# RMS norms without Sqrt: pow on GpSimd, and the FFN's output epilogue spread over four steps

## The chip, the cores and the metric

The kernel runs on all 8 cores of one Trainium2 chip, each with its own part of the batch and no exchange between them. The metric is the device time in microseconds of the slowest core for one execution.

## The reference

One layer of an encoder over 24 sequences (8 and 16 in two batches) of 2048 tokens and width 1024. For each sequence:

```python
h = rms_norm(x, g_mix_pre) * (1 + sc1) + sh1
x = x + gt1 * rms_norm(token_mixer(h), g_mix_post)      # two attention branches, sigmoid gates, w_out
h = rms_norm(x, g_ffn_pre) * (1 + sc2) + sh2
x = x + gt2 * rms_norm(conv_ffn(h), g_ffn_post)         # w_up, conv of width 3, gelu(gate)*val, w_down

def rms_norm(x, g):
    return x * lax.rsqrt(mean(x * x, axis=-1, keepdims=True) + EPS) * g
```

The token mixer is `w_out @ (sigmoid(ga) * ya + sigmoid(gb) * yb)`, where ya and yb are a mixture of three dilated window attentions and a neighbourhood attention on a 32 x 64 grid, 8 heads of 64 each. The FFN has 2816 channels (`D_FF`), so w_up has 5632 columns. Outputs are in float32.

## The kernel before

Each core takes three sequences one after the other (loop over `s`). For each sequence the stages are, with a barrier of all engines between them: the first norm with transposes into `hT` (`ln_to_hT`, four blocks `tcn` of 512 tokens); the two attention branches; the output of the mixer (L746 to L810, four blocks `tcn`); the second norm (`ln_to_hT` again); the FFN (from L826, four blocks `tcn`).

All instructions are recorded by `P.add(engine, ...)` in program order. Each engine executes its own in that order; `reads` and `writes` of the small `Res` objects become semaphore waits of the recorded instruction. A waiting instruction holds up everything recorded behind it on its engine. GpSimd ("pool") has no arithmetic here: its queue holds the weight loads (`wload`, L345), 1 MB of bf16 for eight 128-row pieces of 512 columns. A load waits until the last matmul that reads its slot's former weights is done. Slots come from rings: in the mixer's output `ringC` has three slots and six loads per block (two gate weights at c=0, one at c=2, one at c=4, the two halves of w_out at c=6 and behind c=7); in the FFN `ringF` has four slots, and loads come in pairs (value and gate) at j = 0, 4, 8, 12, 16, 20, then six for w_down.

Mixer output, per block: for c = 0 to 7 TensorE computes ya and yb (L764) and the two gate projections (L781), ScalarE the two Sigmoids (L788, L789), VectorE the products and their sum. Then for each of four 128-token tiles (tt) 16 matmuls with w_out (L807), and `residual_epilogue` (L934) reads the two PSUM halves.

FFN, per block: for j = 0 to 21 TensorE computes the value and the gate half of channel group j (L849, 16 matmuls, two of six PSUM banks); ScalarE scales and biases the middle tap (L866) and mends the block's edges (L871, L875); VectorE adds the two outer taps in place (L881, L885), which frees the banks; one step later come ScalarE's Gelu (L890) and VectorE's product (L892). Then the down-projection (L906) and its copies to SBUF, `RB` (L911). The epilogue of a block is kept in `pend_epi` and recorded in the next block, at j == 3, all four tiles in one go: two Squares with sums (L943), an add (L945), Sqrt (L947), reciprocal (L949), then per half a scaling (L951) and the residual add (L954), and the store of the tile by SP's queue (L920). The first block of a sequence has none pending; the last block's epilogue is recorded at the sequence's end.

`ln_to_hT` has the same pattern per block: four Squares (L434), one Sqrt of 128x4 (L436), reciprocal (L438), four scalings (L440), then 32 transposes (L445). The function tables of ScalarE are switched by the build where the next function isn't in the loaded set: Exp and Ln share one, Sigmoid, Gelu and Sqrt are in others; Square and Identity cause no switch.

Of the kernel before, what the change touches and what calls it, by code (L numbers as in the profile page):

```python
# [6 lines left out]
F32 = mybir.dt.float32  # L7
BF16 = mybir.dt.bfloat16
AF = mybir.ActivationFunctionType
ALU = mybir.AluOpType  # L10
# [4 lines left out]
D = 1024  # L15
NSEQ = 3
NEG = -240000.0
EPS = 1e-6
# [195 lines left out]
def build(debug=False):  # L214
# [16 lines left out]
    P = Prog(nc)  # L231
    A = nc.alloc_sbuf_tensor
# [197 lines left out]
    def ln_to_hT(src_tiles, src_res, tcn, sc_ap, sh_ap, inplace_dst, r_xn):  # L430
        r_ss, r_rs, r_rs2 = r_lnst[tcn % 2]
        so = 4 * (tcn % 2)
        for tt in range(4):
            P.add("act", lambda e, tt=tt: e.activation(out=junk[:], in_=src_tiles[tt], func=AF.Square,  # L434
                                                      accum_out=stat[:, so + tt:so + tt + 1]), reads=[src_res], writes=[r_ss])
        P.add("act", lambda e: e.activation(out=stat[:, 8 + so:12 + so], in_=stat[:, so:so + 4], func=AF.Sqrt, scale=1.0 / D, bias=epsb[:, 0:1]),  # L436
              reads=[r_ss], writes=[r_rs])
        P.add("dve", lambda e: e.reciprocal(out=stat[:, 16 + so:20 + so], in_=stat[:, 8 + so:12 + so]), reads=[r_rs], writes=[r_rs2])  # L438
# [17 lines left out]
    epsb = A("epsb", [128, 1], F32)  # L456
    P.add("dve", lambda e: e.memset(epsb[:], EPS), writes=[r_const])
    r_vec = Res()
    hT_all = [r_hT[j][t] for j in range(8) for t in range(4)]

    def x1tile(i):
        return RA[:, i * D:(i + 1) * D]

    for s in range(nseq):
# [284 lines left out]
        for tcn in range(4):  # L749
# [50 lines left out]
            for tt in range(4):  # L800
                i = tcn * 4 + tt
                pss = []
                for hf in range(2):
                    ps, rps = nb()
                    pss.append((ps, rps))
                    for k in range(8):
                        P.add("pe", lambda e, ps=ps, k=k, tt=tt, hf=hf, wo=wo: e.matmul(  # L807
                            ps[:], lhsT=gT[:, k * 512 + tt * 128:k * 512 + tt * 128 + 128], rhs=wsl(wo[hf][0], k, 512, 0, 512),
                            start=(k == 0), stop=(k == 7)), reads=[r_mg, wo[hf][1]], writes=[rps])
                residual_epilogue(P, pss, x1tile(i), r_x, gt1bc, r_bc, stat, junk, epsb, r_const, Res())  # L810
# [16 lines left out]
        for tcn in range(4):  # L827
            pend = None
            for j in range(22):
# [9 lines left out]
                if j == 3 and pend_epi[0] is not None:  # L839
                    pend_epi[0]()  # L840
                    pend_epi[0] = None
# [71 lines left out]
            def epi(tcn=tcn, s=s, mo_res=mo_res):  # L913
                for tt in range(4):
                    i = tcn * 4 + tt
                    r_y = Res()
                    residual_epilogue(P, [(RB[:, tt * D: tt * D + 512], mo_res[tt]), (RB[:, tt * D + 512: tt * D + 1024], mo_res[tt])],
                                      x1tile(i), Res(), gt2bc, r_bc, stat, junk, epsb, r_const, r_y, sb=True)
                    dsty = bass.AP(y_d, (s * S + i * 128) * D, [[D, 128], [1, D]])
                    P.add("sp", lambda e, dsty=dsty, i=i: e.dma_start(out=dsty, in_=x1tile(i)), reads=[r_y], dma=True)  # L920
            pend_epi[0] = epi
        pend_epi[0]()
# [8 lines left out]
_rst = [None]  # L931


def residual_epilogue(P, halves, xt, r_x, gbc, r_bc, stat, junk, epsb, r_const, r_out, sb=False):  # L934
    if _rst[0] is None:
        _rst[0] = [Res() for _ in range(4)]
# [5 lines left out]
    for hf, (src, rps) in enumerate(srcs):  # L942
        P.add("act", lambda e, src=src, hf=hf: e.activation(out=junk[:, 0:512], in_=src, func=AF.Square,  # L943
                                                            accum_out=stat[:, 32 + c + hf:33 + c + hf]), reads=[rps], writes=[r_st])
    P.add("dve", lambda e: e.tensor_tensor(out=stat[:, 34 + c:35 + c], in0=stat[:, 32 + c:33 + c], in1=stat[:, 33 + c:34 + c], op=ALU.add),  # L945
          reads=[r_st], writes=[r_st])
    P.add("act", lambda e: e.activation(out=stat[:, 35 + c:36 + c], in_=stat[:, 34 + c:35 + c], func=AF.Sqrt, scale=1.0 / D, bias=epsb[:, 0:1]),  # L947
          reads=[r_st, r_const], writes=[r_st])
    P.add("dve", lambda e: e.reciprocal(out=stat[:, 48 + ci:49 + ci], in_=stat[:, 35 + c:36 + c]), reads=[r_st], writes=[r_st])  # L949
# [63 lines left out]
```

How the kernel before makes its waits and increments, by code:

```python
            def run(e, eng):  # L123
                waited = {}
                for x in self.q[e]:
                    for d in x.deps:
                        if d.dma:
                            key = (d.qkey, d.slot)
                            val = d.slotcnt
                            if waited.get(key, 0) >= val:
                                continue
                            waited[key] = val
                            eng.wait_ge(dsem[d.qkey][d.slot], 16 * val)
                        else:
                            key = d.eng
                            val = d.cnt
                            if waited.get(key, 0) >= val:
                                continue
                            waited[key] = val
                            eng.wait_ge(csem[d.eng], val)
                    if x.fn is None:
                        continue
                    bi = x.fn(eng)
                    if x.dma:
                        bi.then_inc(dsem[x.qkey][x.slot], 16)
                    elif x.sig:
                        bi.then_inc(csem[e], 1)
```

## Time and profile before

| what | us |
|---|---|
| median of 2 runs | 5241.87 |
| the two runs | 5103.49 and 5380.25 |
| profiled execution, its own time | 5114.34 |
| its span (slowest core, core 2) | 5112.8 |
| spans of the 8 cores | 5088.2 to 5112.8 |
| busy: TensorE, VectorE, ScalarE, GpSimd | 3720.7, 2231.6, 2419.8, 357.9 |

A time is that of the whole execution; the span runs from the first to the last instruction of a core. All rows are of core 2. PE is TensorE, DVE VectorE, ACT ScalarE, POOL GpSimd, SP the queue of SyncE. In a timeline each row is one or more like instructions in a row; what stands in brackets is how long the engine was idle before them and whose end released it. PEclk is the granted TensorE clock as a share of 2.4 GHz. Some matmul records are missing (63 for 64, say).

### The profile page before, as it was taken

How to read it: one execution, taken by the hardware profiler on the slowest of the kernel's cores; microseconds unless marked ns; L12 is line 12 of the kernel's file. 1: busy time of each engine (PE TensorE's matmuls, PEld its weight loads, DVE VectorE, ACT ScalarE, POOL GpSimd, SP SyncE). 2: the span in 40 equal slices, each digit the busy share in tenths (PEclk: the TensorE clock that was granted, in tenths of full speed). 3: DMA queues.
4: the chain of work that ended last, by engine and by line, in shares of the span. 5: the costliest groups of instructions: out<-in, count | busy, mean ns of one | idle time of the engine just before them, and what ended most of it. 6: DMA issues, size and time to landing. Idle time of an engine off the chain costs nothing.

```text
span 5112.8 us, 67412 instructions; the slowest of 8 cores (5088.2 to 5112.8 us)
## 1 busy us (share of the span) xinstructions
PE 3720.7 (73%) x20982; PEld 1953.1 (38%) x21288; DVE 2231.6 (44%) x3231; ACT 2419.8 (47%) x4878; POOL 357.9 (7%) x417
## 2 busy tenths in 40 slices
PE   1277777795998827777688589973777758958887
PEld 1144444333443324444333344432454433333343
DVE  1444400344566654440034456664543003455665
ACT  0244566224566524556522456652455652245664
POOL 1000000000111000000000011100000000001110
PEclk9689998897999959999889799986999989979998
DMA  8934250521444330000143144433000023224443
GB/s 113 177 50 60 34 75 9 171 99 57 142 149 135 124 122 15 9 13 11 40 142 102 51 152 149 144 112 118 13 7 13 13 64 128 91 66 136 153 149 107
DMA packets 150410, 450.05 MB, mean 88 GB/s; under 512 B 8496, under 2 KB 52528, under 8 KB 149680
## 3 DMA queue, kind: packets, MB, share of 16 engines
q0 software_dynamic: 126160, 356.18, 26.8%
q1 hardware_dynamic: 23904, 89.54, 5.0%
q8 instruction: 182, 2.98, 0.2%
q14 instruction: 164, 1.34, 0.1%
HBM read 468.40 MB, written 57.15 MB: 103 GB/s over the span
## 4 chain that ended last, share of the span: by engine, by line
PE 58%; ACT 14%; issue 9%; DVE 9%; DMA 8%; ACTq 0%; DVEq 0%; POOL 0%; SPq 0%; POOLq 0%
PE pb L849 11%; PE pb L906 9%; PE pb L557 6%; PE pb L781 5%; PE pb L617 5%; PE pb L638 5%; DMA wr<-w_in_bf 5%; PE pb L620 3%; PE pb L807 3%; PE pb L523 3%; PE pb L764 3%; PE pb L445 2%; ACT junk L434 2%; ACT RA L625 2%; DMA RA<-x 2%
## 5 line engine op out<-in xcount | busy, mean ns | idle before, releaser
L625 ACT ACTIVATE RA<-pb 128x448 bf16<-128x448 f32 (+5 forms) x1248 | 543.2, 467 | 269.6 <-PE pb L620 151.3
L617 PE MATMUL pb<-RA 128*128 128x256 bf16 (+4 forms) x2148 | 599.1, 315 | 39.6 <-DVE RA L593 28.9
L881 DVE SCALAR_TENSOR_TENSOR attA<-pb,spt,attA 128x511 f32<-128x511 f32 x528 | 382.5, 747 | 454.9 <-PE pb L849 231.6
L849 PE MATMUL pb<-hT,wr 128*128 128x512 bf16 x2052 | 489.9, 391 | 114.1 <-DVE attA L885 85.4
L638 PE MATMUL pb<-RA 128*128 128x256 bf16 (+5 forms) x2160 | 415.3, 267 | 215.2 <-ACT RA L625 187.3
L849 PE MATMUL pb<-hT,attB 128*128 128x512 bf16 x2067 | 472.6, 382 | 45.4 <-DVE attA L885 42.9
L866 ACT ACTIVATE attA<-pb,spt 128x512 f32<-128x512 f32 x528 | 391.7, 770 | 71.6 <-PE pb L849 70.9
L885 DVE SCALAR_TENSOR_TENSOR attA<-pb,spt,attA 128x511 f32<-128x511 f32 x528 | 368.9, 740 | 0.0
L557 PE MATMUL pb<-hT,wr 128*128 128x512 bf16 x1488 | 359.1, 390 | 8.5 <-ACT RA L547 5.6
L715 DVE TENSOR_TENSOR attB<-pb,RA 64x512 bf16<-64x512 f32 x96 | 66.1, 688 | 655.8 <-ACT RA L713 655.8
L849 PEld LDWEIGHTS pb<-hT,wr 128*128 128x128 bf16 x2112 | 205.3, 100 | 360.2 <-issue 140.8
L638 PEld LDWEIGHTS pb<-RA 128*128 128x128 bf16 x2160 | 193.3, 105 | 366.5 <-issue 308.5
L620 PE MATMUL pb<-Tb,identb 128*128 128x192 bf16 (+2 forms) x1296 | 317.2, 268 | 0.0
L781 PE MATMUL pb<-hT,wr 128*128 128x512 bf16 x1128 | 275.0, 390 | 57.1 <-DMA wr<-w_in_bf 52.8
L849 PEld LDWEIGHTS pb<-hT,attB 128*128 128x128 bf16 x2112 | 203.0, 98 | 283.1 <-issue 51.8
L617 PEld LDWEIGHTS pb<-RA 128*128 128x128 bf16 x2160 | 247.2, 116 | 109.6 <-issue 50.8
L523 PE MATMUL pb<-hT,wr 128*128 128x512 bf16 x744 | 172.2, 389 | 117.0 <-DMA wr<-w_in_bf 106.3
L906 PE MATMUL pb<-wr,RC 128*128 128x512 bf16 x1035 | 235.4, 386 | 15.4 <-DVE attA L885 14.3
L345 POOL DMA_DIRECT2D wr<-w_in_bf x108 | 95.7, 887 | 2105.9 <-PE pb L523 1156.2
L906 PE MATMUL pb<-attB,RC 128*128 128x512 bf16 x1035 | 231.9, 382 | 5.2 <-DVE attA L885 4.1
L911 ACT ACTIVATE RC<-pb 128x512 f32<-128x512 f32 x96 | 57.3, 597 | 374.1 <-PE pb L906 374.1
L668 DVE TENSOR_TENSOR RA<-pb,RA 128x512 f32<-128x512 f32 x96 | 105.8, 1102 | 279.0 <-ACT RA L664 239.0
(130 smaller groups left out, 5447.4 us busy)
## 6 DMA issues: line engine op xcount, KB each, us to landing
wr<-w_up_bf POOLq DMA_DIRECT2D x60, 1024.0 KB, 6.2
attB<-w_up_bf POOLq DMA_DIRECT2D x60, 1024.0 KB, 6.7
RA<-x SPq DMA_DIRECT2D x24, 2048.0 KB, 20.1
wr<-w_in_bf POOLq DMA_DIRECT2D x36, 1024.0 KB, 5.9
wr<-w_down_bf POOLq DMA_DIRECT2D x24, 1024.0 KB, 7.7
attB<-w_down_bf POOLq DMA_DIRECT2D x24, 1024.0 KB, 7.7
y<-RA SPq DMA_DIRECT2D x48, 512.0 KB, 2.6
wr<-w_in_bf POOLq DMA_DIRECT2D x72, 256.0 KB, 3.9
```

The costliest lines, as they stand in the source:

```text
L523: P.add("pe", lambda e, ps=ps, k=k, tcn=tcn, wt=wt: e.matmul(ps[:], lhsT=wsl(wt, k, 128, 0, 128), rhs=hT[:, k * S + tcn * 512:k * S + tcn ...
L557: P.add("pe", lambda e, ps=ps, k=k, tcn=tcn, wt=wt: e.matmul(ps[:], lhsT=wsl(wt, k, 128, 0, 128), rhs=hT[:, k * S + tcn * 512:k * S + tcn ...
L617: P.add("pe", lambda e, ps=ps, col=col, nq=nq, lk=lk, rq=rq: e.matmul(ps[:, col:col + nq], lhsT=lk, rhs=rq, start=True, stop=False, skip_g ...
L620: P.add("pe", lambda e, ps=ps, col=col, nq=nq, mrhs=mrhs: e.matmul(ps[:, col:col + nq], lhsT=identb[:], rhs=mrhs, start=False, stop=True, ...
L625: P.add("act", lambda e, ex=ex, ps=ps, col=col: e.activation(out=ex, in_=ps[:, 0:col], func=AF.Exp, scale=0.125), reads=[rps], writes=[r_e ...
L638: P.add("pe", lambda e, bk=bk, ac0=ac0, nq=nq, lv=lv, exs=exs, first=first: e.matmul(accb[bk][:, ac0:ac0 + nq], lhsT=lv, rhs=exs, start=fi ...
L781: P.add("pe", lambda e, ps_=ps_, w_=w_, k=k, tcn=tcn, c=c: e.matmul(ps_[:], lhsT=wsl(w_, k, 512, (c % 4) * 128, 128), rhs=hT[:, k * S + tc ...
L849: P.add("pe", lambda e, ps=ps, k=k, wt=wt, tcn=tcn, ncol=ncol, jj=jj: e.matmul(ps[:], lhsT=wsl(wt, k, ncol, jj * 128, 128), rhs=hT[:, k * ...
L866: P.add("act", lambda e, t=bufs[isg], ps=mains[isg][0], w1=cw[isg][1], cb=cw[isg][3]: e.activation(out=t, in_=ps[:], func=AF.Identity, sca ...
L881: P.add("dve", lambda e, t=bufs[isg], ps=mains[isg][0], w0=cw[isg][0]: e.scalar_tensor_tensor(out=t[:, 1:512], in0=ps[:, 0:511], scalar=w0 ...
L885: P.add("dve", lambda e, t=bufs[isg], ps=mains[isg][0], w2=cw[isg][2]: e.scalar_tensor_tensor(out=t[:, 0:511], in0=ps[:, 1:512], scalar=w2 ...
L906: P.add("pe", lambda e, ps=ps, k=k, kk=kk, tt=tt, wt=wt: e.matmul(ps[:], lhsT=gT[:, k * 512 + tt * 128:k * 512 + tt * 128 + 128], rhs=wsl( ...
```

## The change

The Sqrt on ScalarE and the reciprocal on VectorE become a `tensor_scalar` on VectorE (times 1/D, plus EPS) and a `tensor_tensor` with `pow` on GpSimd, whose exponent is a small tile `mhalf` of -0.5; in `ln_to_hT` (24 calls) as in `residual_epilogue` (96 calls). The Squares of the epilogues now also write a common resource `r_junk`. The epilogue of an FFN block, recorded in the next one, is no longer all at j == 3 but one tile each at j = 2, 5, 8 and 11. The mixer's epilogues and the one at a sequence's end stay where they are.

```diff
--- before.py
+++ after.py
@@ -433,9 +433,10 @@
         for tt in range(4):
             P.add("act", lambda e, tt=tt: e.activation(out=junk[:], in_=src_tiles[tt], func=AF.Square,
                                                       accum_out=stat[:, so + tt:so + tt + 1]), reads=[src_res], writes=[r_ss])
-        P.add("act", lambda e: e.activation(out=stat[:, 8 + so:12 + so], in_=stat[:, so:so + 4], func=AF.Sqrt, scale=1.0 / D, bias=epsb[:, 0:1]),
-              reads=[r_ss], writes=[r_rs])
-        P.add("dve", lambda e: e.reciprocal(out=stat[:, 16 + so:20 + so], in_=stat[:, 8 + so:12 + so]), reads=[r_rs], writes=[r_rs2])
+        P.add("dve", lambda e: e.tensor_scalar(out=stat[:, 8 + so:12 + so], in0=stat[:, so:so + 4], scalar1=1.0 / D, scalar2=EPS,
+                                               op0=ALU.mult, op1=ALU.add), reads=[r_ss], writes=[r_rs])
+        P.add("pool", lambda e: e.tensor_tensor(out=stat[:, 16 + so:20 + so], in0=stat[:, 8 + so:12 + so], in1=mhalf[:, 0:4], op=ALU.pow),
+              reads=[r_rs, r_const], writes=[r_rs2])
         for tt in range(4):
             P.add("dve", lambda e, tt=tt: e.tensor_scalar(out=inplace_dst[tt], in0=src_tiles[tt], scalar1=stat[:, 16 + so + tt:17 + so + tt],
                                                           scalar2=None, op0=ALU.mult), reads=[src_res, r_rs2], writes=[r_xn])
@@ -454,7 +455,9 @@
                                                                         op0=ALU.mult, op1=ALU.add), reads=[rps, r_vec], writes=[r_hT[j][tcn]])
 
     epsb = A("epsb", [128, 1], F32)
+    mhalf = A("mhalf", [128, 4], F32)
     P.add("dve", lambda e: e.memset(epsb[:], EPS), writes=[r_const])
+    P.add("dve", lambda e: e.memset(mhalf[:], -0.5), writes=[r_const])
     r_vec = Res()
     hT_all = [r_hT[j][t] for j in range(8) for t in range(4)]
 
@@ -807,7 +810,7 @@
                         P.add("pe", lambda e, ps=ps, k=k, tt=tt, hf=hf, wo=wo: e.matmul(
                             ps[:], lhsT=gT[:, k * 512 + tt * 128:k * 512 + tt * 128 + 128], rhs=wsl(wo[hf][0], k, 512, 0, 512),
                             start=(k == 0), stop=(k == 7)), reads=[r_mg, wo[hf][1]], writes=[rps])
-                residual_epilogue(P, pss, x1tile(i), r_x, gt1bc, r_bc, stat, junk, epsb, r_const, Res())
+                residual_epilogue(P, pss, x1tile(i), r_x, gt1bc, r_bc, stat, junk, mhalf, r_const, Res())
         P.barrier()
 
         dump('x1', RA[:])
@@ -836,9 +839,10 @@
                 ffs[0] += 1
                 bufs = (attAf[:, st_ * 1024: st_ * 1024 + 512], attAf[:, st_ * 1024 + 512: st_ * 1024 + 1024])
                 ph, rph = pb[6 + j % 2], rb[6 + j % 2]
-                if j == 3 and pend_epi[0] is not None:
-                    pend_epi[0]()
-                    pend_epi[0] = None
+                if j in (2, 5, 8, 11) and pend_epi[0] is not None:
+                    pend_epi[0]((j - 2) // 3)
+                    if j == 11:
+                        pend_epi[0] = None
                 mains = []
                 for isg in range(2):
                     wt, wr_ = (tv_, tg_)[isg]
@@ -910,16 +914,16 @@
                     ps, rps = pss[tt]
                     P.add("act", lambda e, ps=ps, tt=tt, hf=hf: e.activation(out=RB[:, tt * D + hf * 512: tt * D + hf * 512 + 512], in_=ps[:], func=AF.Identity),
                           reads=[rps], writes=[mo_res[tt]])
-            def epi(tcn=tcn, s=s, mo_res=mo_res):
-                for tt in range(4):
+            def epi(tt_sel, tcn=tcn, s=s, mo_res=mo_res):
+                for tt in ([tt_sel] if tt_sel is not None else range(4)):
                     i = tcn * 4 + tt
                     r_y = Res()
                     residual_epilogue(P, [(RB[:, tt * D: tt * D + 512], mo_res[tt]), (RB[:, tt * D + 512: tt * D + 1024], mo_res[tt])],
-                                      x1tile(i), Res(), gt2bc, r_bc, stat, junk, epsb, r_const, r_y, sb=True)
+                                      x1tile(i), Res(), gt2bc, r_bc, stat, junk, mhalf, r_const, r_y, sb=True)
                     dsty = bass.AP(y_d, (s * S + i * 128) * D, [[D, 128], [1, D]])
                     P.add("sp", lambda e, dsty=dsty, i=i: e.dma_start(out=dsty, in_=x1tile(i)), reads=[r_y], dma=True)
             pend_epi[0] = epi
-        pend_epi[0]()
+        pend_epi[0](None)
         pend_epi[0] = None
         P.barrier()
     P.barrier()
@@ -931,9 +935,10 @@
 _rst = [None]
 
 
-def residual_epilogue(P, halves, xt, r_x, gbc, r_bc, stat, junk, epsb, r_const, r_out, sb=False):
+def residual_epilogue(P, halves, xt, r_x, gbc, r_bc, stat, junk, mhalf, r_const, r_out, sb=False):
     if _rst[0] is None:
-        _rst[0] = [Res() for _ in range(4)]
+        _rst[0] = [Res() for _ in range(5)]
+    r_junk = _rst[0][4]
     ci = _ctr[0] % 4
     c = ci * 4
     _ctr[0] += 1
@@ -941,12 +946,13 @@
     srcs = [(ps if sb else ps[:], rps) for (ps, rps) in halves]
     for hf, (src, rps) in enumerate(srcs):
         P.add("act", lambda e, src=src, hf=hf: e.activation(out=junk[:, 0:512], in_=src, func=AF.Square,
-                                                            accum_out=stat[:, 32 + c + hf:33 + c + hf]), reads=[rps], writes=[r_st])
+                                                            accum_out=stat[:, 32 + c + hf:33 + c + hf]), reads=[rps], writes=[r_st, r_junk])
     P.add("dve", lambda e: e.tensor_tensor(out=stat[:, 34 + c:35 + c], in0=stat[:, 32 + c:33 + c], in1=stat[:, 33 + c:34 + c], op=ALU.add),
           reads=[r_st], writes=[r_st])
-    P.add("act", lambda e: e.activation(out=stat[:, 35 + c:36 + c], in_=stat[:, 34 + c:35 + c], func=AF.Sqrt, scale=1.0 / D, bias=epsb[:, 0:1]),
+    P.add("dve", lambda e: e.tensor_scalar(out=stat[:, 35 + c:36 + c], in0=stat[:, 34 + c:35 + c], scalar1=1.0 / D, scalar2=EPS,
+                                           op0=ALU.mult, op1=ALU.add), reads=[r_st], writes=[r_st])
+    P.add("pool", lambda e: e.tensor_tensor(out=stat[:, 48 + ci:49 + ci], in0=stat[:, 35 + c:36 + c], in1=mhalf[:, 0:1], op=ALU.pow),
           reads=[r_st, r_const], writes=[r_st])
-    P.add("dve", lambda e: e.reciprocal(out=stat[:, 48 + ci:49 + ci], in_=stat[:, 35 + c:36 + c]), reads=[r_st], writes=[r_st])
     for hf, (src, rps) in enumerate(srcs):
         P.add("dve", lambda e, src=src, hf=hf: e.scalar_tensor_tensor(out=src, in0=src, scalar=stat[:, 48 + ci:49 + ci],
                                                                    in1=gbc[:, hf * 512:(hf + 1) * 512], op0=ALU.mult, op1=ALU.mult),
```

## Rows read from the trace of the kernel before

**Rows 1.** Page, chain that ended last: share of span by engine.
```profile
PE 58%; ACT 14%; issue 9%; DVE 9%; DMA 8%; ACTq 0%; DVEq 0%; POOL 0%; SPq 0%; POOLq 0%
```

**Rows 2.** ScalarE by line: name, shape, count | busy us, mean ns | idle.
```profile
L947 ACT ACT_TABLE_LOAD x24 | 30.8, 1283 | 15.3 <-DVE stat L945 15.3
...
L788 ACT ACT_TABLE_LOAD x12 | 15.4, 1283 | 95.3 <-PE pb L781 95.2
L890 ACT ACT_TABLE_LOAD x12 | 15.4, 1283 | 0.2
L436 ACT ACTIVATE stat<-stat,epsb 128x4 f32<-128x4 f32 x24 | 7.1, 297 | 2.8
```

**Rows 3.** Waits: who waited <- for whom: us total, times, longest.
```profile
PE pb L849 <- DVE attA L885: 128.2, 9, 14.6
```

**Rows 4.** Timeline, second FFN block: start, duration us, engine, line [idle <-releaser].
```profile
3032.14 13.98 PE L849 MATMUL pb<-hT,attB 128*128 128x512 bf16 x63
...
3037.49 1.51 DVE L881 SCALAR_TENSOR_TENSOR attA<-pb,spt,attA 128x511 f32<-128x511 f32 x2 [37.85 <-PE pb L849]
...
3040.95 1.51 DVE L881 SCALAR_TENSOR_TENSOR attA<-pb,spt,attA 128x511 f32<-128x511 f32 x2 [0.63 <-ACT attA L875]
...
3047.74 0.15 DVE L945 TENSOR_TENSOR stat<-stat 128x1 f32<-128x1 f32 x1
...
3049.66 0.16 DVE L949 RECIPROCAL stat<-stat 128x1 f32<-128x1 f32 x1 [1.77 <-ACT stat L947]
...
3053.95 0.75 DVE L951 SCALAR_TENSOR_TENSOR RC<-RC,stat,gt2bc 128x512 f32<-128x512 f32 x1
...
3057.06 0.15 DVE L945 TENSOR_TENSOR stat<-stat 128x1 f32<-128x1 f32 x1
...
3065.47 1.40 DVE L881 SCALAR_TENSOR_TENSOR attA<-pb,spt,attA 128x511 f32<-128x511 f32 x2
...
3067.67 9.94 PE L849 MATMUL pb<-hT,wr 128*128 128x512 bf16 x32 [14.64 <-DVE attA L885]
...
3091.26 9.01 PE L849 MATMUL pb<-hT,wr 128*128 128x512 bf16 x40
```

**Rows 5.** A stretch of that block: busy us by engine, PEclk, DMA.
```profile
3060.00:3075.00 15.00, 7.33 (x21) 2.73 (x22) 13.79 (x22) 12.63 (x26) 0.00 (x0) 0.55 0.18 71
```

**Rows 6.** Timeline of TensorE, third FFN block, after a short stall.
```profile
3260.51 15.66 PE L906 MATMUL pb<-wr,RC 128*128 128x512 bf16 x63 [4.05 <-DVE attA L885]
```

**Rows 7.** Timeline, GpSimd's weight-load issues in the block of rows 4.
```profile
3032.84 0.88 POOL L345 DMA_DIRECT2D wr<-w_up_bf  x1 [4.28 <-PE pb L906]
...
3076.43 0.88 POOL L345 DMA_DIRECT2D wr<-w_up_bf  x1 [28.88 <-PE pb L849]
```

**Rows 8.** DMA issues: count, KB each, median us from issue to landing.
```profile
wr<-w_up_bf POOLq DMA_DIRECT2D x60, 1024.0 KB, 6.2
...
wr<-w_in_bf POOLq DMA_DIRECT2D x36, 1024.0 KB, 5.9
```

**Rows 9.** Timeline, first mixer output block meeting the second.
```profile
2615.96 0.88 POOL L345 DMA_DIRECT2D wr<-w_in_bf  x1 [0.91 <-PE pb L781]
...
2624.74 0.16 DVE L945 TENSOR_TENSOR stat<-stat 128x1 f32<-128x1 f32 x1 [6.49 <-ACT junk L943]
...
2630.01 0.15 DVE L945 TENSOR_TENSOR stat<-stat 128x1 f32<-128x1 f32 x1
...
2633.03 0.88 POOL L345 DMA_DIRECT2D wr<-w_in_bf  x1 [16.18 <-PE pb L807]
...
2635.72 1.89 PE L781 MATMUL pb<-hT,wr 128*128 128x512 bf16 x8
...
2639.21 1.89 PE L781 MATMUL pb<-hT,wr 128*128 128x512 bf16 x8 [1.60 <-DMA wr<-w_in_bf]
```

**Rows 10.** GpSimd by line, columns as in rows 2.
```profile
L361 POOL DMA_DIRECT2D w_down_bf<-w_down x2 | 2.5, 1248 | 0.0
...
L215 POOL MEMSET const-float32-0.0<- 128x1 f32 x1 | 0.1, 98 | 0.5 <-issue 0.5
```

## The prediction, made before the changed kernel was run

> **What bounds the kernel now.** I began with the page's chain of work that ended last: TensorE holds 58% of it, ScalarE 14%, VectorE 9%, DMA 8%, GpSimd nothing [rows 1]. So the Sqrts matter only where TensorE ends up waiting for an epilogue. Next the grouped lines of ScalarE: the loads of function tables are 24 at L947, 12 at L788 and 12 at L890, 1.283 us each [rows 2]. Without Sqrt, the Sigmoid and Gelu tables are needed once per sequence instead of once per block of 512 tokens: all 24, 9 of 12 and 9 of 12 go, and one before L436, together 43 x 1.283 = 55 us of ScalarE. Then the list of waits, for TensorE in the FFN: it waits for VectorE's L885 nine times, 128.2 us in all [rows 3]. Nine is the number of FFN blocks that have a pending epilogue (three of four in each of three sequences). The timeline of one such block shows it [rows 4]: TensorE starts j=0 at 3032.14 (call it T) and needs 13.98 us for 64 matmuls, 3.50 per j. VectorE handles one j per 3.46 us (3037.49, 3040.95), so **VectorE is as full as TensorE** and can't make up lost time while the up-projection runs. At T+15.6 the four epilogues begin, and the next convolution (j=3) starts at 3065.47: 17.7 us in which no PSUM bank comes free. TensorE uses up its lead of six banks, stands 14.64 us, and its next 32 matmuls take 9.94 us instead of 7.0: the granted clock was 0.55 on average from 3060 to 3075 [rows 5], mostly its lower level of 1.2 GHz, after TensorE had been idle. j=12 starts at 3091.26 = T+59.1.
>
> **One thing in the profile is easy to pass over: GpSimd is the queue of the weight loads.** Each load is one instruction there that waits until its slot is free; behind it nothing moves, and it moves for nothing ahead of it. Now they are issued early: the weights of j=4 at 3032.84, those of j=12 at 3076.43, the latter 14.8 us ahead of their use [rows 7]; from issue to landing a load takes 6.2 us [rows 8]. The pow of the change is put into this queue.
>
> **FFN blocks, 9 times.** Price of one epilogue on VectorE: the four together took 17.73, of that 1.28 a table load, so 4.11 each; 3.11 of it are the four wide operations (3053.95 to 3057.06), 1.00 the small ones with their handoffs. I take off Sqrt (0.29) and reciprocal (0.16), add a tensor_scalar of about 0.15 (as the add of L945) with 0.1 of handoff, and the pow, L: 3.9 + L. Four are 15.6 + 4L against 17.7. ScalarE no longer waits for VectorE here; its two Squares (1.6 us) hide behind the 3.9 + L. Spreading them over j=2, 5, 8, 11 wins little by itself, since VectorE has only 0.04 us of slack per j in between.
>
> Now the loads. The epilogue at j=2 starts where the convolution of j=2 would, T+5.35+6.92 = T+12.3; its pow ends at T+12.8+L; only then can the weights of j=4 be issued, and they land at T+19.0+L, while TensorE wants them at T+14. It stands for 5+L us. A stall of 4.05 us is enough to cost clock: 63 matmuls took 15.66 instead of 13.8 us after it [rows 6]. With some 2.5 us for that (between 1.9 and 2.9) and the 1.84 us from matmul to convolution, VectorE gets j=4 at T+26.8+L instead of T+23.1+L, 3.7 late. The weights of j=8 wait for the pow at j=5 and land near their use; VectorE is the later one there. The last pow, at j=11, ends at T + 5.35 + 11x3.46 + 3(3.9+L) + 0.5 + L + 3.7 = T+59.3+4L. **Behind it stands the load for j=12**: it lands at T+65.5+4L, long after TensorE has finished j=11. Against T+59.1 of today that is 6.4+4L, and 2.5 for the clock. Behind j=12 nothing is late: VectorE has the rest of its epilogue and j=11 done by then, and the later loads (j=16 on) stand behind no pow. In return the short wait in each sequence's third block may go (4.05 + 1.9 of clock, once in three blocks, 2.0 on average). Sum: **7 + 4L per block, 9(7+4L)**.
>
> **Mixer output blocks, 9 boundaries.** Today the first gate-weight load of the next block is issued at 2615.96, before the epilogues, the second at 2633.03; TensorE starts the gate groups at 2635.72 and 2639.21, the second 1.60 us late [rows 9]. Now both stand behind four pows. First epilogue: its add at 2624.74, the next at 2630.01, 5.27 with a table load, 3.99 without; by the same exchange 3.8 + L. The fourth pow ends at 2624.74 + 0.5 + L + 3(3.8+L) = 2636.6+4L. The load lands 5.9 us later [rows 8], 2642.5+4L; the second group starts 1.9 after that, at 2644.4+4L against 2639.21: 5.2+4L, and about 2 for the clock after a stall of 6.8+4L. **Again 7 + 4L, 9 times.** The 1.28 us of Sqrt table at the start of this chain are counted in; the Sigmoid table fell into the wait for the DMA and gives nothing, and would be 1.28 x 9 = 12 us more if that cover were not there. The other table loads lie beside TensorE's work.
>
> **The rest.** In the 24 norms Sqrt (0.30 at L436 [rows 2]) and reciprocal become tensor_scalar and pow: L - 0.2 each, all on the path, as TensorE has nothing else there. Six places where four epilogues end before a barrier (mixer and FFN, once per sequence each): 15.6+4L against 17.7, 4L - 2.1 each. The junk dependency orders Squares that are in order on one engine already; the memset is one instruction: nothing.
>
> **The pow itself** is in no row. Nearest from below: GpSimd's memset of the same 128x1, 0.098 us; from above: its longest instruction, a DMA issue of 1.248 us [rows 10]. I take 0.5: the tile is that of the memset, the work more. Sum: 2x9x(7+4L) + 24(L-0.2) + 6(4L-2.1) = 109 + 120L, **+169 us at L = 0.5**, +121 at 0.1, +259 at 1.25. The profiled execution took 5114.3 us (span 5112.8), so 5283, with 5235 and 5373 as bounds. That execution lies at the lower of the two runs shown (5103.49); the median with the other is 5241.87. I forecast on the level of the profiled one.
>
> The Trainium skill (ScalarE: Activation LUTs, What ACT_TABLE_LOAD costs) puts a switch of tables at 1.28 us for the load and another 1.38 of draining, which would speak for the change. Here the row that waits for the first Sqrt shows 1.77 us before L949 [rows 4], which leaves about 0.5 beside the 1.28; no drain of 1.38 fits in. By the page the 18 first Sqrts on the path would give back 25 us more and the sum would be 5258. The Trainium skill (GPSIMD Engine Reference, Instruction dispatch) also has a first call of newly loaded GpSimd code wait about 6 us; no row shows it, and by it the sum would be 5289.
>
> **The rivals.**
> *Faster: the stall dissolves.* Spread out, each epilogue fits into TensorE's lead of banks and no bank is late: 9 x (14.2 + 2.7) = 152 us less, 4962 if the loads land in time, 5043 (-1.4%) if the mixer's 81 us are paid. For it: the 14.64 us come from a burst. Against: it decides only if VectorE needs at most (3x3.50 - 3.9 - L)/3 = 2.0 us per j, and it needs 3.46. Chance 0.07 for the first, 0.05 for the second.
> *Only one stage pays.* The late loads cost nothing in the FFN because VectorE has held TensorE up by as much: only the mixer's 81 and the 7 us of the rest stay, 5202 (+1.7%). For it: until j=11 VectorE is the later one. Against: at j=12 the load follows the pow, and cannot be hidden. 0.16.
> *A slow pow.* GpSimd needs 2.5 us: 109 + 300, 5523. For it: it is a power, not a fill. Against: nothing in the rows. 0.08.
>
> **How the numbers follow.** 0.64 for the forecast. The comparison can tell about 2% from no change (5012 to 5217). Faster 0.07; same 0.05 + 0.16 = 0.21; slower 0.64 + 0.08 = 0.72. The range takes the bounds of L, reaches down to the one-stage case and leaves out the two far ones: 5180 to 5385.
>
> **What would show it.** In the trace after: 10 table loads in place of 53; GpSimd rows of pow and their duration L; the weight load for j=12 starting right behind the pow of j=11, with a wait of TensorE for DMA wr<-w_up_bf of 10 us or so in each of 9 blocks, and of 5 us at j=4; waits of TensorE for DMA w_in_bf of 7 us or more at 9 mixer boundaries; L849's waits for L885 split into short ones. I am wrong if the loads start before the pows, if L is far from 0.5, or if the granted clock does not fall after these stalls.

## The result, and the profile after

The changed kernel is slower: 5339.29 us median of 11 runs, and 1.0437 times the time of the kernel before, 95% interval 1.0398 to 1.0476. Its profiled execution took 5326.85 us, with a span of 5325.3 on its slowest core (core 1), against 5112.8 before: 212.5 us more. Ratios compare executions in which no die's clock was disturbed (the kernel before took 5103 to 5148 us in those, beside these 11), and since the profiled executions of e6 and e9 had one die at a lower clock, their stage times are medians over the four cores of the other die.

Where the time went shows when each stage is measured alone. The numbers below are worked out from the two traces: the time from a stage's first instruction to that of the next, median of the eight cores, summed over the three sequences (for the norms the two of a sequence, for the FFN its blocks, are taken one by one and added). The differences add up to 216, the spans of the slowest cores differ by 212.5.

```
stage, us                                  before     after   difference
start, before the first norm                148.6     150.3      +1.7
the two norms, 24 blocks                    509.7     532.1     +22.4
attention branches                         1907.5    1909.1      +1.6
mixer output, 9 block boundaries            842.3     922.4     +80.1
FFN block 0 (no epilogue pending)           384.5     385.6      +1.1
FFN blocks 1 to 3, and the last epilogue   1305.0    1414.5    +109.5
```

The page's chain by engine has DMA at 12% where it was 8% [rows 1]:

```profile
PE 57%; DMA 12%; ACT 10%; DVE 10%; issue 9%; POOL 1%; DVEq 0%; ACTq 0%; SPq 0%; POOLq 0%
```

The list of waits names the loads. TensorE waited for the w_up loads 3 times, once per sequence, before; now 33 times. The one group of nine waits for VectorE [rows 3] is gone; what the list puts down to VectorE and ScalarE now is shown below. At the gate projections (L784, formerly L781) it now waits 123.9 us for w_in. First the line of the kernel before, then those of the changed one:

```profile
PE pb L849 <- DMA wr<-w_up_bf: 25.7, 3, 9.5
```

```profile
PE pb L784 <- DMA wr<-w_in_bf: 123.9, 27, 9.8
...
PE pb L853 <- DMA wr<-w_up_bf: 93.0, 20, 12.7
...
PE pb L853 <- DMA attB<-w_up_bf: 43.3, 13, 12.9
DVE pb L957 <- POOL stat L954: 41.8, 48, 1.2
...
PE pb L853 <- DVE RC L896: 34.0, 5, 11.8
...
PE pb L853 <- ACT attA L894: 29.2, 8, 6.1
```

The fourth line is VectorE's wait for the pow in the mixer's epilogues, 0.87 us each. The last two are TensorE's and name another engine, but mean the loads too. Outside the three starts of an FFN, TensorE on this core stands for more than 2 us 26 times in the up-projection, and each of these waits ends 0.35 us after a w_up load has landed (one of them 0.51 us), whatever its row names: in each of the nine blocks 5.3 to 7.9 us at j=4 and 8.6 to 12.9 us at j=12, and in eight of them 2.1 to 5.7 us at j=8.

GpSimd's new rows give the unknown of the sum: the pow of 128x1 takes 0.548 us, that of 128x4 1.010:

```profile
L954 POOL TENSOR_TENSOR stat<-stat,mhalf 128x1 f32<-128x1 f32 x96 | 52.7, 548 | 947.3 <-DVE stat L952 947.3
...
L438 POOL TENSOR_TENSOR stat<-stat,mhalf 128x4 f32<-128x4 f32 x24 | 24.2, 1010 | 402.3 <-DVE stat L436 369.4 <-DMA attB<-G 33.0
```

And ScalarE's table loads are 10 in all, where 53 were:

```profile
L628 ACT ACT_TABLE_LOAD x3 | 3.8, 1283 | 11.3 <-PE pb L623 11.3
L791 ACT ACT_TABLE_LOAD x3 | 3.8, 1283 | 92.4 <-PE pb L784 59.8 <-DMA wr<-w_in_bf 32.6
L894 ACT ACT_TABLE_LOAD x3 | 3.8, 1283 | 0.1
...
L404 ACT ACT_TABLE_LOAD x1 | 1.3, 1283 | 29.3 <-DVE RA L384 29.3
```

The timeline of the FFN block that answers to [rows 4, 7] (second block of sequence 1, T = 3138.33) shows the mechanism. Each pow is followed at once by the loads that stood behind it: the pair for j=4 (wr) after the first, the pairs for j=12 (wr) and j=16 (attB) after the fourth. TensorE's two restarts at 3158.03 and 3205.28 wait for exactly these (the rows between them, left out here, have one more wait, 2.19 us for j=8):

```profile
3138.33 13.98 PE L853 MATMUL pb<-hT,attB 128*128 128x512 bf16 x64
...
3151.03 0.56 POOL L954 TENSOR_TENSOR stat<-stat,mhalf 128x1 f32<-128x1 f32 x1 [22.89 <-DVE stat L952]
...
3151.59 1.80 POOL L345 DMA_DIRECT2D wr<-w_up_bf  x2
...
3158.03 3.57 PE L853 MATMUL pb<-hT,wr 128*128 128x512 bf16 x8 [5.73 <-DMA wr<-w_up_bf]
...
3198.31 0.54 POOL L954 TENSOR_TENSOR stat<-stat,mhalf 128x1 f32<-128x1 f32 x1 [13.47 <-DVE stat L952]
...
3198.86 1.81 POOL L345 DMA_DIRECT2D wr<-w_up_bf  x2
...
3200.66 1.76 POOL L345 DMA_DIRECT2D attB<-w_up_bf  x2
...
3205.28 3.57 PE L853 MATMUL pb<-hT,wr 128*128 128x512 bf16 x8 [11.40 <-DMA wr<-w_up_bf]
```

j=12 starts at T+66.95; before it was T+59.1. TensorE alone, from there on, and two stretches of the windows view (busy us by engine, then PEclk, share of the DMA engines, GB/s):

```profile
3209.82 14.58 PE L853 MATMUL pb<-hT,wr 128*128 128x512 bf16 x56 [0.97 <-ACT attA L870]
3224.24 13.98 PE L853 MATMUL pb<-hT,attB 128*128 128x512 bf16 x64
```

```profile
3177.00:3205.00 28.00, 15.90 (x64) 6.36 (x64) 25.57 (x43) 19.41 (x44) 4.65 (x6) 0.81 0.32 111
3205.00:3213.00 8.00, 6.75 (x16) 2.21 (x17) 0.39 (x1) 0.78 (x1) 0.00 (x0) 0.50 1.03 367
```

From 3205 to 3213 the granted clock is 0.50, the lower level of 1.2 GHz, after 11.4 us of idleness, and the DMA engines are full (367 GB/s), since four 1 MB loads were issued within 3.6 us. The gate half of j=12 is late too: issued at 3199.78, it lands at 3209.47, and TensorE goes on at 3209.82, after 0.97 us of standing. (The row puts this down to an ACTIVATE of ScalarE, which ended at the same moment.) The 64 matmuls of j=12 to 15 take until 3224.24, 18.96 us instead of the 13.82 of before (3091.26 to 3105.08): 5.1 more, of which 0.97 is this wait and 4.2 the lower clock. 7.8 us at the start of j=12 and 5.1 after it are the 12.9 by which this block is longer.

The mixer's boundary that answers to [rows 9]: the add of the first epilogue, its pow, the fourth pow, the two loads behind it, and TensorE standing 9.16 us:

```profile
2704.97 0.16 DVE L950 TENSOR_TENSOR stat<-stat 128x1 f32<-128x1 f32 x1 [6.49 <-ACT junk L948]
...
2705.54 0.57 POOL L954 TENSOR_TENSOR stat<-stat,mhalf 128x1 f32<-128x1 f32 x1 [10.26 <-DVE stat L952]
...
2718.26 0.54 POOL L954 TENSOR_TENSOR stat<-stat,mhalf 128x1 f32<-128x1 f32 x1 [3.66 <-DVE stat L952]
2718.87 1.80 POOL L345 DMA_DIRECT2D wr<-w_in_bf  x2
...
2725.28 5.88 PE L784 MATMUL pb<-hT,wr 128*128 128x512 bf16 x16 [9.16 <-DMA wr<-w_in_bf]
```

### The profile page after: what moved, and what is told of

The parts are those of the page before. It is cut to its first block, busy times and chain, and to the rows that moved or that the text cites. A ratio compares the mean times of both kernels' runs of the same rounds, so it can differ in the third digit from the quotient of the medians.

```text
span 5325.3 us, 67917 instructions; the slowest of 8 cores (5293.2 to 5325.3 us)
## 1 busy us (share of the span) xinstructions
PE 3805.9 (71%) x21288; PEld 1967.8 (37%) x21288; DVE 2225.1 (42%) x3232; ACT 2340.9 (44%) x4715; POOL 435.9 (8%) x537
## 4 chain that ended last, share of the span: by engine, by line
PE 57%; DMA 12%; ACT 10%; DVE 10%; issue 9%; POOL 1%; DVEq 0%; ACTq 0%; SPq 0%; POOLq 0%
PE pb L853 12%; PE pb L910 9%; PE pb L560 6%; PE pb L784 6%; PE pb L620 5%; DMA wr<-w_in_bf 5%; PE pb L641 4%; PE pb L623 3%; PE pb L767 2%; PE pb L526 2%; DMA wr<-w_up_bf 2%; PE pb L446 2%; ACT RA L628 2%; DMA wr<-w_ada 1%; ACT junk L434 1%
## 5 line engine op out<-in xcount | busy, mean ns | idle before, releaser
L620 PE MATMUL pb<-RA 128*128 128x256 bf16 (+5 forms) x2160 | 605.9, 316 | 39.6 <-DVE RA L596 28.9
L853 PE MATMUL pb<-hT,wr 128*128 128x512 bf16 x2112 | 515.0, 401 | 145.7 <-DMA wr<-w_up_bf 93.0
L641 PE MATMUL pb<-RA 128*128 128x256 bf16 (+5 forms) x2160 | 418.0, 269 | 215.3 <-ACT RA L628 192.6
L853 PE MATMUL pb<-hT,attB 128*128 128x512 bf16 x2112 | 492.6, 390 | 78.9 <-DMA attB<-w_up_bf 43.3
L784 PE MATMUL pb<-hT,wr 128*128 128x512 bf16 x1152 | 292.7, 408 | 123.9 <-DMA wr<-w_in_bf 123.9
L560 PE MATMUL pb<-hT,wr 128*128 128x512 bf16 x1536 | 365.6, 391 | 5.9 <-DMA wr<-w_in_bf 3.2
L853 PEld LDWEIGHTS pb<-hT,wr 128*128 128x128 bf16 x2112 | 207.1, 101 | 417.0 <-issue 211.1
L718 DVE TENSOR_TENSOR attB<-pb,RA 64x512 bf16<-64x512 f32 x96 | 66.1, 688 | 653.7 <-ACT RA L716 622.9
L526 PE MATMUL pb<-hT,wr 128*128 128x512 bf16 x768 | 179.0, 393 | 110.8 <-DMA wr<-w_in_bf 104.3
L910 PE MATMUL pb<-wr,RC 128*128 128x512 bf16 x1056 | 236.8, 386 | 13.3 <-DVE attA L889 13.3
L784 PEld LDWEIGHTS pb<-hT,wr 128*128 128x128 bf16 x1152 | 116.6, 103 | 288.2 <-issue 173.1
```

The source lines that it names most:

```text
L526: P.add("pe", lambda e, ps=ps, k=k, tcn=tcn, wt=wt: e.matmul(ps[:], lhsT=wsl(wt, k, 128, 0, 128), rhs=hT[:, k * S + tcn * 512:k * S + tcn ...
L560: P.add("pe", lambda e, ps=ps, k=k, tcn=tcn, wt=wt: e.matmul(ps[:], lhsT=wsl(wt, k, 128, 0, 128), rhs=hT[:, k * S + tcn * 512:k * S + tcn ...
L620: P.add("pe", lambda e, ps=ps, col=col, nq=nq, lk=lk, rq=rq: e.matmul(ps[:, col:col + nq], lhsT=lk, rhs=rq, start=True, stop=False, skip_g ...
L641: P.add("pe", lambda e, bk=bk, ac0=ac0, nq=nq, lv=lv, exs=exs, first=first: e.matmul(accb[bk][:, ac0:ac0 + nq], lhsT=lv, rhs=exs, start=fi ...
L784: P.add("pe", lambda e, ps_=ps_, w_=w_, k=k, tcn=tcn, c=c: e.matmul(ps_[:], lhsT=wsl(w_, k, 512, (c % 4) * 128, 128), rhs=hT[:, k * S + tc ...
L853: P.add("pe", lambda e, ps=ps, k=k, wt=wt, tcn=tcn, ncol=ncol, jj=jj: e.matmul(ps[:], lhsT=wsl(wt, k, ncol, jj * 128, 128), rhs=hT[:, k * ...
```

## The experiments

The theory after the result (**queue**): weight loads stand behind pows in GpSimd's queue and are issued too late. Rivals: VectorE's **round trip** to GpSimd is what costs; the **spreading** of the FFN epilogue is what costs. The stage times of all runs stand in one table at the end of this section.

### Loads in another queue: e7, with its control e3

All bf16 weight loads go to SP's queue and the stores of y to GpSimd's; e7 does this to the changed kernel, e3 to the kernel before. The pows of e7 stay where they are.

```diff
-        P.add("pool", lambda e, dst=dst, src=src: e.dma_start(out=dst, in_=src), reads=deps, writes=[sl.res], dma=True)
+        P.add("sp" if deps else "pool", lambda e, dst=dst, src=src: e.dma_start(out=dst, in_=src), reads=deps, writes=[sl.res], dma=True)
...
-                    P.add("sp", lambda e, dsty=dsty, i=i: e.dma_start(out=dsty, in_=x1tile(i)), reads=[r_y], dma=True)
+                    P.add("pool", lambda e, dsty=dsty, i=i: e.dma_start(out=dsty, in_=x1tile(i)), reads=[r_y], dma=True)
```

> The changed kernel with its bf16 weight loads moved from GpSimd's queue to SP's, and the stores of y from SP's to GpSimd's. The pows stay on GpSimd, at the same places. Theory (queue): what costs is that weight loads stand behind pows. With the loads elsewhere the 80 us of the mixer and most of the 109 us of the FFN go; the 22 us of the norms and the 0.55 us round trips stay: 5105 to 5160, ratio to the kernel before 1.00 to 1.01. Rival (round trip): what costs is VectorE waiting for GpSimd; nothing changes for it, ratio 1.03 to 1.045. Rival (spreading): the FFN's 109 us stay, ratio about 1.025.

> The control: the kernel before, with Sqrt, and only the queues swapped as in e7 (weight loads on SP's, stores of y on GpSimd's). Every theory expects no change beyond 1% (ratio 0.99 to 1.01), unless the other queue itself lands loads faster or later; then e7 is to be read against this run.

e7: ratio 0.9918 (0.9900 to 0.9936). e3: 0.9876 (0.9855 to 0.9897). The waits of e7:

```profile
PE pb L853 <- DVE attA L889: 88.1, 36, 3.9
...
PE pb L853 <- DMA wr<-w_up_bf: 22.5, 3, 9.0
...
PE pb L784 <- DMA wr<-w_in_bf: 8.5, 16, 1.3
```

With the same pows on the same engine, TensorE waits for w_up only at the three FFN starts, 22.5 us, and for w_in 8.5 us in place of 123.9. Of 4.4% loss nothing is left; the ratio is even below the 1.00 to 1.01 expected, by what the other queue gains in e3. Read against e3, as its expectation demands, the change costs e7 0.4%: 25 us in the norms (526.1 against 500.8) less 8 in the FFN (1298.8 against 1307.0), nothing in the mixer (781.1 against 781.5). The round trip is still there 96 times in e7, so it isn't the cause. The control missed its expectation: the swap of queues alone gains 1.2%, of which 61 us are in the mixer (below).

### Loads recorded ahead of the pow: e4, e11, e12

Here the queue stays, and only the order in it changes, in the FFN alone: e4 records the pairs of j=4, 8 and 12 before the epilogues at j=2, 5 and 11; e11 only that of j=12, e12 only those of j=4 and 8.

```diff
                 if jj == 0:
-                    tv_ = wload(...)
-                    tg_ = wload(...)
+                    if j in early:
+                        tv_, tg_ = early.pop(j)
+                    else:
+                        tv_, tg_ = up_pair(j)
+                if tcn > 0 and j in (2, 5, 11):        # e11: j == 11; e12: j in (2, 5)
+                    early[(j // 4 + 1) * 4] = up_pair((j // 4 + 1) * 4)
```

> The changed kernel, but in the FFN the pairs of weight loads for j=4, 8 and 12 are recorded ahead of the epilogues at j=2, 5 and 11, so that they stand before the pow in GpSimd's queue. Pow, spreading, mixer and norms as changed. Queue: the FFN's 109 us go (VectorE's insertion is 15.6+4x0.55=17.8 us per block, as before), the mixer's 80 and the norms' 22 stay: about 5210, ratio 1.015 to 1.025. Round trip or spreading: the FFN keeps its 109 us, ratio 1.04.

> The changed kernel with one pair of loads of the FFN recorded ahead of a pow, that of j=12 at j=11; those of j=4 and j=8 stay behind the pows of j=2 and j=5. If the load for j=12 is what decides, as the prediction says, the greater part of the FFN's 109 us goes: what is left is the late j=4 (3.7 us per block by the sum), about 5240, ratio 1.022 to 1.030. If the late j=4 decides: above 1.035.

> The complement of e11: the pairs of j=4 and j=8 ahead of the pows at j=2 and j=5, that of j=12 behind the pow of j=11. By the sum only the 3.7 us of j=4 go per block, 33 us in all: ratio 1.035 to 1.040. If j=4 decides: 1.025 or less.

e4: ratio 1.0175 (1.0153 to 1.0197); e11: 1.0289 (1.0260 to 1.0319); e12: 1.0351 (1.0266 to 1.0437). In e4 the FFN falls from 1414.5 to 1284.0 us, 21 below the kernel before (only its 109 us were expected to go), while mixer and norms keep their loss. What TensorE waits for in e4's up-projection (L865 there) is VectorE again, in short waits:

```profile
PE pb L865 <- DVE attA L901: 69.9, 37, 3.9
...
PE pb L865 <- DMA wr<-w_up_bf: 27.9, 5, 9.7
```

By stages, the load of j=12 alone gives back 86.0 us, those of j=4 and 8 alone 50.2, together 130.5. So the last one decides, and the early ones count for more than the 3.7 us per block of the sum: 1328.5 - 1284.0 = 44.5 us, 4.9 per block, remain in e11.

### The other part of the change alone: e2 and e1

e2 has the pows but not the spreading (`if j == 3: pend_epi[0](None)`); e1 has the spreading but keeps Sqrt and reciprocal.

> The changed kernel without the spreading: all four epilogues at j=3, with pow on GpSimd. Queue: the loads of j=4 stand behind four pows, the fourth ends near T+30, they land near T+37; TensorE starts j=4 then where it started j=6 at T+35.5 before: 9 to 12 us per block, as in the changed kernel; mixer and norms as changed. Ratio 1.035 to 1.045. Spreading as the cause: FFN back to the time before, 5215, ratio 1.02.

> The kernel before, Sqrt and reciprocal kept, with only the spreading of the FFN epilogue over j=2, 5, 8, 11. Queue: no pow, so no load is late; but each of the four epilogues now switches to the Sqrt table and back, so VectorE's insertion is about 5.4 us and more each, 22 to 26 against 17.7 us per block: 4 to 9 us more, ratio 1.007 to 1.016. If spreading dissolves the stall: ratio 0.97. If spreading is what costs the changed kernel its 109 us in the FFN: ratio 1.02 or more.

e2: 1.0394 (1.0376 to 1.0413). e1: 1.0060 (1.0040 to 1.0080). The FFN of e2 is 79.4 us above the kernel before (8.8 per block, where 9 to 12 were expected), without any spreading, and its waits are long ones for the loads behind four pows, 21.6 to 24.7 us in each of the nine blocks. Four of them are put down to VectorE's L895 in the list, but these too end 0.35 us after a w_up load has landed:

```profile
PE pb L852 <- DMA wr<-w_up_bf: 118.1, 11, 23.8
...
PE pb L852 <- DVE RC L895: 89.3, 4, 22.8
```

The FFN of e1 is 23.6 us above it, less than the 36 to 81 expected, though each of its epilogues switches tables twice (51 loads at its Sqrt and 39 at its Gelu, against 24 and 12). So spreading by itself costs a little with Sqrt. With pow, and loads on time, the FFN is 21 us shorter than before (e4); how much of this is the spreading is not shown, for want of a run with pow at j=3 and its loads on time. With the loads behind the pows, spreading makes two restarts out of one and costs 30 us more than the burst (1414.5 against 1384.4). e1 and e4 both spread and both have their loads on time, and e4's FFN is 44.6 us shorter, 1.24 for each of 36 epilogues: about the 1.28 us of one table load, which here VectorE has to wait for. e4 also issues its loads earlier; the two were not taken apart.

### A dose: e5, every pow twice

```diff
+    P.add("pool", lambda e: e.tensor_tensor(out=stat[:, 48 + ci:49 + ci], in0=stat[:, 35 + c:36 + c], in1=mhalf[:, 0:1], op=ALU.pow),
+          reads=[r_st, r_const], writes=[r_st])
```

behind the pow of the epilogue, and the same behind that of the norm.

> The changed kernel with every pow executed twice on GpSimd, one after the other, into the same place. A dose test: 0.65 us more for each of 96 epilogues (0.55 and a handoff), 1.1 for each of 24 norms. Queue: the slope of the sum, (36+36+24) x 0.65 + 24 x 1.1 = 62 + 26 = 88 us above the changed kernel, ratio to the kernel before 1.055 to 1.065. If the pow's duration did not matter (only that a load is in a queue with one): under 30 us above it, ratio 1.045.

```profile
L956 POOL TENSOR_TENSOR stat<-stat,mhalf 128x1 f32<-128x1 f32 x96 | 52.3, 545 | 945.3 <-DVE stat L954 945.3
L958 POOL TENSOR_TENSOR stat<-stat,mhalf 128x1 f32<-128x1 f32 x96 | 52.2, 543 | 14.4 <-POOL stat L956 0.9
```

Ratio 1.0665 (1.0569 to 1.0762), just above the 1.055 to 1.065 expected and not to be told from it; the profiled execution took 5406.8 us, 80 above the changed kernel's, where 88 were expected. By stages: mixer +39.0, FFN +28.3 (by the slope about 31 each), norms +9.5 where 26 were expected. The slope of the two stages in which loads stand behind pows is right. In the norms the second pow is on the path as expected: from the end of the last Square's sum to the first scaling, the 24 blocks take 66.1 us together where the changed kernel takes 39.2 (median of the cores), 26.9 more. But the transposes that follow take 134.0 us together where they took 146.6, 12.6 less, at a mean granted clock of 0.65 against 0.60. So the clock gave back about half; why it was granted higher is not shown, and the other 5 us of the difference are not traced.

### The mixer alone: e6

The kernel before, with tensor_scalar and pow in place of Sqrt and reciprocal in `residual_epilogue` if `sb` is False, that is in the mixer.

> The kernel before with pow on GpSimd in the mixer's epilogues alone; norms and FFN keep Sqrt, the FFN epilogue stays at j=3. Queue: the mixer's part alone, +80 us, ratio 1.014 to 1.017, FFN and norms unchanged. Rival (the mixer's part is a consequence of something else, such as SP's or the clock): under 20 us, ratio 1.00.

Ratio 1.0173 (1.0149 to 1.0198). The mixer takes 929.4 us, 87 more; FFN 1301.7 and norms 514.5 hardly move. The mixer's part is its own.

### Is VectorE what stops TensorE at j=6? e9

The kernel before, with the pending epilogue recorded where VectorE is idle:

```diff
-                if j == 3 and pend_epi[0] is not None:
-                    pend_epi[0]()
-                    pend_epi[0] = None
...
             pend[0]()
             pend[1]()
+            if pend_epi[0] is not None:
+                pend_epi[0]()
+                pend_epi[0] = None
             mo_res = r_mo
```

> The kernel before with the pending FFN epilogue recorded at the start of the down-projection instead of at j=3, Sqrt kept. There VectorE has nothing to do for some 37 us. If the stall of TensorE at j=6 comes from VectorE being full during the up-projection (as the prediction read it), the 14.2 + 2.7 us per block go in 9 blocks: 110 to 152 us less, ratio 0.970 to 0.979. If the stall only moves to the banks of the down-projection: ratio 0.99 to 1.00.

Ratio 0.9739 (0.9672 to 0.9806). FFN blocks 1 to 3 take 1151.2 us, 153.8 less than before; (14.2 + 2.7) x 9 is 152. Core 4's waits, all that are left in the FFN's matmuls but for 2.1 us in the small ones for the block edges:

```profile
PE pb L846 <- DMA wr<-w_up_bf: 22.9, 3, 7.7
...
PE pb L906 <- DVE attA L882: 17.7, 8, 4.2
```

The nine waits of [rows 3] are gone, and none came in their place. So the stall was there to be had; spreading over the up-projection looks for room where VectorE has none, the down-projection has it.

### Both together: e10 and e8

e10 is the kernel before with the edits of e3 and e9; e8 is the same with the change's pow and `junk` resource.

> The kernel before with both rearrangements that helped: the FFN epilogue at the start of the down-projection (ratio 0.974 alone) and the weight loads in SP's queue, the stores in GpSimd's (0.988 alone). They act in different stages, so they should add: ratio 0.955 to 0.967, about 4900.

> As e10, but with the change's pow on GpSimd in place of Sqrt. By the queue theory a pow costs only its round trip once no load stands behind it: the norms' 22 us remain, the four epilogues before barriers and the down-projection are free of it: ratio 0.96 to 0.97, at most 0.6% above e10. If pow on GpSimd harms by other ways: 1% or more above e10.

e10: ratio 0.9588 (0.9560 to 0.9616), 4901.53 us median, the fastest of all. e8: 0.9665 (0.9623 to 0.9707). The two edits add (0.9739 x 0.9876 = 0.9618). By stages e10 has the 60 us of e3 in the mixer; its FFN gains 144 us, 10 less than e9's, all of it lost in or after the last block of a sequence. e8 stands 0.8% above e10, a little more than the 0.6% expected: 23 us in the norms and 9 in the FFN, mostly after its last block, where four epilogues end before a barrier.

```
us, three sequences        norms   mixer   FFN 1-3   ratio to before
before                     509.7   842.3   1305.0    1
after (the change)         532.1   922.4   1414.5    1.0437
e1 spreading alone         511.2   841.9   1328.6    1.0060
e2 pow alone, at j=3       533.7   921.4   1384.4    1.0394
e3 queues swapped, Sqrt    500.8   781.5   1307.0    0.9876
e4 FFN loads first         534.2   928.9   1284.0    1.0175
e5 pow twice               541.6   961.4   1442.8    1.0665
e6 pow in mixer alone      514.5   929.4   1301.7    1.0173
e7 change, queues swapped  526.1   781.1   1298.8    0.9918
e8 e7, epilogue in down    524.6   785.1   1170.6    0.9665
e9 Sqrt, epilogue in down  509.6   843.9   1151.2    0.9739
e10 e3 and e9 together     501.3   782.7   1161.4    0.9588
e11 only j=12 first        534.0   925.0   1328.5    1.0289
e12 only j=4, j=8 first    533.1   922.6   1364.3    1.0351
```

## Why the prediction was right, and where it was wrong

**Direction and mechanism were right.** Slower, because loads stand behind pows: e7 takes the loads out of the queue and the loss is gone, e4 turns the order round in the FFN and the FFN's loss is gone. The signs named beforehand came too: waits of 5.3 to 7.9 us at j=4 ("5 us"), of 8.6 to 12.9 at j=12 ("10 us or so"), 9.16 at the mixer's boundary ("7 us or more").

**The size was wrong**: the sum said +169 us on 5114.3, a ratio of 1.033; measured were +212.5 us between the profiled executions and 1.0437. Two terms of the sum were too small: the nine FFN blocks, 81 us in the sum and 109.5 measured, and the 24 norms, 7 in the sum and 22.4 measured. The mixer's 81 was right, 80.1. Placed on the level of the profiled execution, 5283 was moreover only 0.8% above the median then shown, 5241.87, which is the middle between a run at that level and one of 5380.25; against that number the forecast reads as hardly any loss, and the ratio measured is 4.4%. The measured median of 5339.29 lies inside the range, in its upper half; that was luck, owed to the wide bounds for the pow, up to 1.25 us, and not to the terms that were missed. Term by term:

- *L*, taken as 0.5 between 0.098 and 1.248: 0.548 measured. That is worth 6 us, no more. That the norm's pow has four columns and takes 1.010 us was missed: one L stood for both. The timeline of a norm block has 1.44 us from tensor_scalar to scaling, where the kernel before has 0.68 from Sqrt to scaling. Counted from the end of the last Square's sum, which now has a handoff to VectorE behind it, the 24 norms take 39.2 us in place of 20.5, and the transposes behind them 146.6 in place of 139.6, at a mean granted clock of 0.60 against 0.63. So **the norms' term, L - 0.2 each, is a step that failed**: 22.4 us instead of 24 x 0.3 = 7.

```profile
2943.22 0.17 DVE L436 TENSOR_SCALAR stat<-stat 128x4 f32<-128x4 f32 x1 [5.78 <-ACT junk L434]
2943.54 1.01 POOL L438 TENSOR_TENSOR stat<-stat,mhalf 128x4 f32<-128x4 f32 x1 [9.29 <-DVE stat L436]
2944.66 3.33 DVE L441 TENSOR_SCALAR RC<-RA,stat 128x1024 f32<-128x1024 f32 x4 [1.26 <-POOL stat L438]
```

- *Mixer*: 9(7+4L) with L = 0.548 is 83, measured 80.1 (with the stage's tail). The fourth pow ends 13.8 us after the first add (14.1 by the sum with this L), TensorE starts 6.4 us after the load behind it was issued (5.9), and stands 9.16 us (9.0).
- *FFN, up to j=12*: the first pow ends at T+13.3 (12.8+L = 13.35), j=4 starts at T+19.7 (19.55), the last pow ends at T+60.5 (61.5), j=12 starts at T+66.95 (67.7). Every step of the working holds within 1 us, but for j=8: there the sum had VectorE as the later one, and TensorE waited 2.1 to 5.7 us for the load in eight of nine blocks. That may be why the early loads counted for more than 3.7 us per block (e11); it was not taken apart.
- *FFN, after j=12* is **the step that failed**, with more of the miss than any other: "Behind j=12 nothing is late" and "2.5 for the clock". The sum went by one load of 6.2 us, the median, but j=12 needs a pair: its first half landed 6.07 us after its issue, the gate half 9.7 us after its own. TensorE stood another 0.97 us for it, and the lower clock cost 4.2 us instead of 2.5, together 5.1. The pair of j=16 was issued in the same breath as that of j=12, and the median landing rose from 6.2 us to 8.1 for the w_up loads into wr, from 6.7 to 9.0 for those into attB. That the four loads together made the gate half late is not shown: the second load of a pair took 8.5 us in the kernel before and 9.25 at j=4, with no second pair behind it. First the line of before, then those of the changed kernel:

```profile
attB<-w_up_bf POOLq DMA_DIRECT2D x60, 1024.0 KB, 6.7
```

```profile
wr<-w_up_bf POOLq DMA_DIRECT2D x60, 1024.0 KB, 8.1
attB<-w_up_bf POOLq DMA_DIRECT2D x60, 1024.0 KB, 9.0
```

- *FFN, third block*: I credited 2.0 us per block for a short wait of the down-projection that would go. It stayed, 4.05 us in the third block of sequence 1 as in [rows 6]; that block is 39.7 us longer over the three sequences, the second 36.3, the fourth with the epilogue behind it 33.4.

```profile
3391.54 8.75 PE L910 MATMUL pb<-wr,RC 128*128 128x512 bf16 x32 [4.05 <-DVE attA L889]
```

This and the step above make 9 x (2.6 + 2.0) = 41 us of the miss; 0.8 us that j=12 came earlier than worked out take 7 back. That makes 34 us where 109.5 - 83 = 26.5 are missing; these steps were read in one block, and the other 8 us are what the blocks differ by from it.
- *The stall dissolves* (the rival, 0.07 and 0.05) did not happen. With the loads on time (e4) the one stall per block turns into about four short ones, 37 waits for VectorE of up to 3.9 us, as the reason given had it: VectorE needs 3.46 us per j. e9 shows that the 152 us of its price were there (153.8), only not to be had by spreading.
- *Only one stage pays* (0.16) fell with the stage table: both pay. *A slow pow* (0.08) fell with 0.548.
- *Table loads*: 10 in place of 53, as forecast. In the changed kernel no stage gains by it; it may be what makes e4's FFN 44.6 us shorter than that of e1, where VectorE waits for the table load of each Sqrt. The Trainium skill (ScalarE: Activation LUTs, What ACT_TABLE_LOAD costs) adds 1.38 us of draining to each; by [rows 4] there was no room for it.
- The Trainium skill (GPSIMD Engine Reference, Instruction dispatch) has the first call of newly loaded code wait about 6 us. Here the first pow of the program runs 1.04 us and starts 0.32 us after the tensor_scalar before it began, as the later ones: this case shows no such wait.

## What to carry to other kernels

An instruction is priced by its engine's queue, not by its engine's load: GpSimd was 7% busy, and 0.64 us of work in it (76.9 us for 120 calls) cost 1.8 us of the kernel for every call (212.5 / 120), in the main because the weight loads of the next step stood behind it and behind all that it waits for. Before putting arithmetic on an engine that issues prefetches, list what is recorded behind it, or record those loads first (e4), or give them a queue in which nothing waits for the epilogues (e7). And when a side task must find room on a full engine, look for the phase in which that engine is idle (e9), not for gaps in the phase that fills it.

## What the hardware showed that I had not expected

- The same loads from SP's queue, with only the stores of y moved the other way (e3), gained 1.2%, 61 us of it in the mixer. TensorE's waits for w_in at the gate projections were 52.8 us before and are 11.3 in e3, and the 2 MB loads of x, now ahead of the weights in the same queue, land after 10.6 us (median) instead of 20.1. The line of the kernel before, then that of e3:

```profile
PE pb L781 <- DMA wr<-w_in_bf: 52.8, 25, 5.6
```

```profile
PE pb L781 <- DMA wr<-w_in_bf: 11.3, 14, 2.1
```

Whether this is the order of x and weights, or the queue itself, was not taken apart. The queue itself does differ: the same 450.05 MB went in 440714 DMA packets in e3, in 150410 before, and the w_up loads into wr land after 5.7 us (median) instead of 6.2.

- A pow on GpSimd takes 0.544 us for one column of 128 partitions and 1.010 for four (medians); by these two sizes a further column costs an estimated 0.155 us. The memset there takes 0.098.
- A stall of TensorE is paid twice: in the 8 us shown after the 11.4 us one, the granted clock was at its lower level throughout, and that cost the matmuls of j=12 to 15 4.2 us.
